# First weights in halves, squares shared with ScalarE, page numbers moved, and a new order at the end of the feed-forward: a one-core decoder layer

## What is computed

```python
xn = rms_norm(x, g)                       # x: 256 + 32 rows of 1024
z  = einsum('btd,de->bte', xn, w_in)      # the combined projection, then split into q, k, v, gates
...                                       # two attention branches over paged caches, found by page_table
h  = merge_branches(...)
hn = rms_norm(h, norm_ffn_g)
u, g = hn @ w_up, hn @ w_gate             # 3072 columns each
uc = conv_b + sum(conv_w[k] * ue[:, k:k + T] for k in range(3))
y  = h + (gelu(uc) * g) @ w_down          # out: y_prompt, y_sample
conv_rows = ue[:, -2:]                    # out: p_conv, s_conv, the last two rows of u
```

## Time and profile before

| | us |
|---|---|
| median of 3 runs (lowest, highest) | 930.73 (930.58, 931.37) |
| the profiled execution, its own time | 936.61 |
| its span, first to last instruction | 933.8 |
| PE busy in the span | 865.1 (93%) |
| DVE busy | 525.0 (56%) |
| ACT busy | 367.8 (39%) |
| GpSimd (POOL) busy | 160.9 (17%) |
| granted TensorE clock, mean over the span | 0.974 |

### The profile page before, as it was taken

How to read it: one execution, slowest core, us unless ns; L and a number is a source line. 1 busy time by engine, 2 the same in 40 slices (tenths; PEclk the granted TensorE clock), 3 DMA queues, 4 the chain that set the end, 5 groups by cost and what they waited for, 6 DMA issues and landing times. The chain is left out here.

```text
span 933.8 us, 18057 instructions
## 1 busy us (share of the span) xinstructions
PE 865.1 (93%) x7225; PEld 709.6 (76%) x7225; DVE 525.0 (56%) x981; ACT 367.8 (39%) x662; POOL 160.9 (17%) x262
## 2 busy tenths in 40 slices
PE   3999878799999999999999977999979999999996
PEld 2888667689989977655656455997678988989884
DVE  5466578633434566754467434656656655666554
ACT  3336565432434323453224422434144434444330
POOL 1200041311121022233434510000010110101000
PEclk9999989999999899999999999999979999999999
DMA  5543096165424269989999995974064444564412
GB/s 173 182 165 109 14 313 234 56 149 131 173 93 182 91 249 395 325 319 411 414 416 420 385 407 155 300 243 160 9 207 145 146 135 140 200 194 140 135 45 60
DMA packets 90608, 191.89 MB, mean 205 GB/s; under 512 B 7434, under 2 KB 68650, under 8 KB 78154
## 3 DMA queue, kind: packets, MB, share of 16 engines
q0 software_dynamic: 15408, 106.04, 29.3%
q1 hardware_dynamic: 73836, 84.43, 29.2%
q10 hardware_dynamic: 1296, 0.45, 0.2%
HBM read 187.44 MB, written 7.64 MB: 209 GB/s over the span
## 5 line engine op out<-in xcount | busy, mean ns | idle before, releaser
L1587 PEld LDWEIGHTS banks<-consts_base,stream_rows 128*128 128x128 f32 x672 | 73.2, 141 | 31.0 <-issue 27.3
L1834 ACT ACTIVATE keys_turned<-banks 128x512 f32<-128x512 f32 x94 | 54.9, 596 | 100.3 <-PE banks L1587 100.2
L258 PE MATMUL banks<-tokens_turned_high,w_gates_high 128*128 128x288 f32 x288 | 86.6, 301 | 3.5 <-PEq L191 2.3
L1587 PE MATMUL banks<-consts_base,stream_rows 128*128 128x128 f32 x672 | 82.5, 275 | 4.7 <-PEq L191 1.7
L259 PE MATMUL banks<-tokens_turned_low,w_gates_high 128*128 128x288 f32 x288 | 85.6, 297 | 0.0
L1126 PE MATMUL banks<-chunks_turned_high,cmp_w_high 64*128 64x256 f32 (+1 forms) x512 | 78.5, 300 | 5.3 <-DVE cmp_w_low L251 2.7
L260 PE MATMUL banks<-tokens_turned_high,w_gates_low 128*128 128x288 f32 x272 | 81.8, 301 | 0.0
L1126 PE MATMUL banks<-chunks_turned_low,cmp_w_high 64*128 64x256 f32 (+1 forms) x512 | 75.3, 288 | 0.0
L1126 PE MATMUL banks<-chunks_turned_high,cmp_w_low 64*128 64x256 f32 (+1 forms) x512 | 75.1, 287 | 0.0
L1815 DVE COPY keys_turned<-banks 128x512 f32<-128x512 f32 x74 | 50.4, 690 | 29.6 <-PE banks L1587 27.1
L251 DVE TENSOR_TENSOR chunks_turned_low<-banks,chunks_turned_high 128x512 fp32r<-128x512 f32 x64 | 41.1, 684 | 41.3 <-ACT chunks_turned_high L246 41.3
(11 more groups left out here) (446 smaller groups left out, 2110.1 us busy)
## 6 DMA issues: line engine op xcount, KB each, us to landing
w_up_gate<-in_w_up SPq DMA_DIRECT2D x12, 1024.0 KB, 7.4
w_up_gate<-in_w_gate SPq DMA_DIRECT2D x12, 1024.0 KB, 9.9
w_down<-in_w_down SPq DMA_DIRECT2D x12, 1024.0 KB, 5.0
w_in_slot<-in_w_in SPq DMA_DIRECT2D x8, 1424.0 KB, 6.3
w_gates<-in_w_in SPq DMA_DIRECT2D x10, 512.0 KB, 7.5
cmp_w<-in_cmp_w_k SPq DMA_DIRECT2D x4, 512.0 KB, 8.7
cmp_w<-in_cmp_w_v SPq DMA_DIRECT2D x4, 512.0 KB, 11.4
stream_rows<-in_state_win_k SPq DMA_DIRECT2D x8, 256.0 KB, 8.8
```

What stands on the lines that cost most here:

```text
L258: nc.tensor.matmul(out, lh, rh, start=start, stop=False, **kw)
L1587: ins = nc.tensor.transpose(bank(t)[:, q * P:(q + 1) * P], src, ident)
L1834: copy = lambda a, b: nc.scalar.activation(a, b, ACT.Copy)
```

## The change

1. Tokens: the squares of tiles 1 and 2 are made by ACT (Square with an accumulated sum) and those of tile 0 by DVE. ACT's order is squares 1, root 0, root 1, squares 2, root 2.
2. The first block of weights is loaded as two halves, and its high part is made at the start of the projection, by halves, each followed by DVE's low half.
3. The eight loads of page numbers go from ACT's list in the tokens stage to SP's in the projection, behind block 1.
4. End of the feed-forward: `down_sample` comes ahead of the last `down`; DVE adds each prompt tile as soon as its two banks are done, and SP stores it; the six groups of new rows go through six banks, and ACT copies four of them out.

```diff
@@ stage_tokens, sync
-            load_w_in(c, sp, w, w_loaded, 0, ORDER[0] * ZC)
+            for half in range(2):
+                src = c.d["w_in"].rearrange("l (k p) e -> p (l k) e", p=P)[:, half * KD // 2:(half + 1) * KD // 2, bass.ds(ORDER[0] * ZC, ZC)]
+                sp.dma_start(first_half(w[0], half), src).then_inc(w_first[half], 16)
@@ stage_tokens, scalar
-            with nc.allow_non_contiguous_dma(reason="1024 page numbers"):
-                for b in range(DB):
-                    src = bcast(d["page_table"][b, :], 1, 8)
-                    act.dma_start(c.pages[:, b:b + 1], src.unsqueeze(2)).then_inc(pages_in, 16)
-            for t in range(3):
-                act.wait_ge(squared, t + 1)
+            def squares(t):
+                act.wait_ge(tokens_in[t], 16)
+                nc.scalar.activation(xn[0:rows[t], t, :], x[0:rows[t], t, :], ACT.Square, scale=D ** -0.5,
+                                     accum_out=ss[0:rows[t], t:t + 1]).then_inc(squared[t], 1)
+            def root(t):
+                act.wait_ge(squared[t], 1)
                 nc.scalar.activation(ss[0:rows[t], t:t + 1], ss[0:rows[t], t:t + 1], ACT.Sqrt,
                                      bias=c.eps[0:rows[t], :]).then_inc(root_ready, 1)
+            act.wait_ge(eps_ready, 1)
+            squares(1)
+            root(0)
+            root(1)
+            squares(2)
+            root(2)
...
-            act.wait_ge(w_loaded[0], 16)
-            split_high(nc, wh[0][:, :, :], w[0][:, :, :]).then_inc(high, 1)
@@ stage_project, sync
             load_w_in(c, sp, w, w_loaded, 1, at(1))
+            with nc.allow_non_contiguous_dma(reason="1024 page numbers"):
+                for b in range(DB):
+                    src = bcast(d["page_table"][b, :], 1, 8)
+                    sp.dma_start(c.pages[:, b:b + 1], src.unsqueeze(2)).then_inc(c.pages_in, 16)
@@ stage_project, scalar
+            for half in range(2):
+                act.wait_ge(w_first[half], 16)
+                split_high(nc, first_half(wh[0], half), first_half(w[0], half)).then_inc((first_high, high)[half], 1)
@@ stage_project, vector
-            dve.wait_ge(high, 1)
             for half in range(2):
+                dve.wait_ge((first_high, high)[half], 1)
+                split_low(nc, first_half(wl[0], half), first_half(w[0], half), first_half(wh[0], half)).then_inc((first_low, low)[half], 1)
@@ stage_ffn, sync
+            for t in range(QT):
+                sp.wait_ge(y_ready, 2 * t + 2)
+                sp.dma_start(d["y_prompt"].rearrange("b (t p) d -> p (b t) d", p=P)[:, t, :], h[:, t, :]).then_inc(c.stored, 16)
             sp.wait_ge(y_ready, 6)
-            sp.dma_start(d["y_prompt"].rearrange("b (t p) d -> p (b t) d", p=P), h[:, 0:2, :]).then_inc(c.stored, 16)
@@ stage_ffn, tensor, after the loop
+            pe.wait_ge(dn_low, FT)
+            pe.wait_ge(hid_ready, FT)
+            down_sample(1, False)
             pe.wait_ge(hid_low, FT)
-            pe.wait_ge(dn_low, FT)
-            down(1, False)
-            down_sample(1, False)
+            down(1, False, rows_done)
...
             for g in range(FT // 4):
-                pe.wait_ge(kept, FT)
-                if g >= 2:
-                    pe.wait_ge(lcopy, g - 1)
+                if g in (2, 4):
+                    pe.wait_ge(y_ready, g)
                 for k in range(4):
-                    ins = nc.tensor.transpose(c.ps[g % 2][0:NL, k * P:(k + 1) * P], last[:, 4 * g + k, :], c.k("ident"))
+                    ins = nc.tensor.transpose(c.ps[g][0:NL, k * P:(k + 1) * P], last[:, 4 * g + k, :], c.k("ident"))
@@ stage_ffn, scalar, after the loop
+            for g in (0, 1, 2, 4):
+                act.wait_ge(lturn, g + 1)
+                nc.scalar.activation(last_rows[:, g * 512:(g + 1) * 512], c.ps[g][0:NL, :], ACT.Copy).then_inc(lcopy, 1)
@@ stage_ffn, vector
+                else:
+                    dve.wait_ge(rows_done, t + 1)
...
-            for g in range(FT // 4):
+            for g in (3, 5):
```

More of the change, by code:

```diff
@@ L273, in load_w_in, with first_half, stage_tokens @@
     sp.dma_start(w[u][:, :, :], c.d["w_in"].rearrange("l (k p) e -> p (l k) e", p=P)[:, :, bass.ds(start, ZC)]).then_inc(loaded[u], 16)
-def stage_tokens(c, z_at, w, w_loaded, wh, high):
+def first_half(x, half):
+    return x[:, half * KD // 2:(half + 1) * KD // 2, :]
+def stage_tokens(c, z_at, w, w_first):
     nc, d = c.nc, c.d
@@ L287, in stage_tokens @@
         high_ready = c.sem("xT_high_ready")
-        pages_in, squared, root_ready = c.pages_in, c.sem("x_squared"), c.sem("x_root_ready")
+        squared, root_ready, eps_ready = [c.sem(f"x_squared{t}") for t in range(3)], c.sem("x_root_ready"), c.sem("eps_ready")
         rows = [P, P, NS]
@@ L323, in _ @@
             link = c.chain(dve, "vector")
[L324 to L329, removed]
+            nc.vector.memset(c.eps[:, :], EPS).then_inc(eps_ready, 1)
+            dve.wait_ge(tokens_in[0], 16)
+            nc.vector.tensor_tensor_reduce(xn[:, 0, :], x[:, 0, :], x[:, 0, :], 1.0 / D, 0.0,
+                                           ALU.mult, ALU.add, ss[:, 0:1]).then_inc(squared[0], 1)
             dve.wait_ge(gain_in, 16)
@@ L356, with stage_project @@
 ORDER = (3, 4, 5, 6, 0, 1, 2, 7)
-def stage_project(c, z, w, w_loaded, wh, wl, high, chunks):
+def stage_project(c, z, w, w_first, w_loaded, wh, wl, chunks):
     nc, d = c.nc, c.d
@@ L377, in stage_project @@
         qgain = c.sb("q_gains_by_partition", [P, 2], ctx=ctx)
+        high, first_high = c.sem("w_in_high_ready"), c.sem("w_in_first_high_ready")
         low, first_low = c.sem("w_in_low_ready"), c.sem("w_in_first_low_ready")
+        loads = lambda n: 16 * (n // 2 + n % 2)
         z_out = [c.sem(f"z_copied_{e}") for e in "va"]
@@ L483, in _ @@
                     pe.wait_ge(fold_out, n - 1)
-                pe.wait_ge(w_loaded[u], n // 2 * 16 + 16)
+                if n:
+                    pe.wait_ge(w_loaded[u], loads(n))
                 for k in range(KD):
                     g = k % 4
+                    if n == 0 and k % 4 == 0:
+                        pe.wait_ge(w_first[k // 4], 16)
                     m = nc.tensor.matmul(U[3 * u + 2][32 * g:32 * g + 32, 0:ZC], c.xsT[:, k, :], w[u][:, k, :], start=(k < 4), stop=(k >= 4))
@@ L518, in split @@
                 u = n % 2
-                act.wait_ge(w_loaded[u], n // 2 * 16 + 16)
+                act.wait_ge(w_loaded[u], loads(n))
                 if n >= 2:
@@ L2529, in _, with down @@
             loop(sp, FT // 4, body)
+            for t in range(QT):
+                sp.wait_ge(y_ready, 2 * t + 2)
+                sp.dma_start(d["y_prompt"].rearrange("b (t p) d -> p (b t) d", p=P)[:, t, :], h[:, t, :]).then_inc(c.stored, 16)
             sp.wait_ge(y_ready, 6)
-            sp.dma_start(d["y_prompt"].rearrange("b (t p) d -> p (b t) d", p=P), h[:, 0:2, :]).then_inc(c.stored, 16)
             sp.dma_start(d["y_sample"].rearrange("b s d -> (b s) d"), h[0:NS, 2, :]).then_inc(c.stored, 16)
-            sp.wait_ge(lcopy, FT // 4)
+            sp.wait_ge(lcopy, 4)
+            sp.wait_ge(lcopy_late, 2)
             sp.dma_start(d["p_conv"].rearrange("l b w f -> (l b w) f"), last_rows[0:2, :]).then_inc(c.stored, 16)
             sp.dma_start(d["s_conv"].rearrange("l b w f -> (l b w) f"), last_rows[2:NL, :]).then_inc(c.stored, 16)
-            sp.wait_ge(c.stored, 16 * (c.n_stored + 4))
+            sp.wait_ge(c.stored, 16 * (c.n_stored + 5))
         @block.tensor
         def _(pe):
-            def down(f, start):
+            def down(f, start, rows_done=None):
                 for t in range(QT):
@@ L2546, in down @@
                                       start=start, stop=True, skip_group_check=True)
-                ins.then_inc(down_done, 1)
+                    if rows_done:
+                        ins.then_inc(rows_done, 1)
+                if not rows_done:
+                    ins.then_inc(down_done, 1)
             def down_sample(u, start):
@@ L2772, in build @@
                     wl = [c.at("w_in_low0", [P, KD, ZC], F32R, 8 * NH * SEQ), c.in_big("w_in_low1", [P, KD, ZC], F32R, 0)]
-                    w_loaded, high = [c.sem(f"w_in_loaded{u}") for u in range(2)], c.sem("w_in_high_ready")
-                    stage_tokens(c, z_at, w, w_loaded, wh, high)
-                    stage_project(c, z, w, w_loaded, wh, wl, high, chunks)
+                    w_loaded, w_first = [c.sem(f"w_in_loaded{u}") for u in range(2)], [c.sem(f"w_in_first_loaded{u}") for u in range(2)]
+                    stage_tokens(c, z_at, w, w_first)
+                    stage_project(c, z, w, w_first, w_loaded, wh, wl, chunks)
                 stage_prompt(c, z, chunks)
```

6 lines of the change are left out of this document (3 added, 3 removed).

## The result

| | before | changed |
|---|---|---|
| median of 20 runs, taken together (lowest, highest) | 931.66 (930.58, 936.35) | 937.20 (931.67, 939.51) |
| ratio of the times, 95% interval | | 1.0031 (1.0018 to 1.0043) |
| the profiled execution, own time | 936.61 | 937.52 |
| its span | 933.8 | 935.8 |
| PE busy | 865.1 | 866.6 |

The changed kernel is slower by 0.31%, 2.9 us of 932, where 929.6 was forecast. Its median is outside the range, and the sign is the other one. The sign is sure and the size less so: over these 20 runs of each the means differ by 3.7 and the medians by 5.5, because the times of the kernel before fall in two groups (of 35 runs taken together, 13 took 930.16 to 932.54 and 22 took 934.42 to 937.17, with none between), and a median depends on how many runs fell in which. The three runs shown ahead of the prediction are all in the range of the lower group.

A forecast was written before the change was run, and what follows sets the result against it. PE's path, block 2's chain to the row numbers close behind it, and DVE's path to the last store bound the kernel. Front +1.5 and end -2.6 made -1.1, from 930.73 to 929.6; range 927.2 to 932.4.

The forecast's parts named there:

- What bounds the kernel: Whole program: PE, busy 93% of the span, bounds it; only its path or the path to the last store counts.
- the front: Program start through PE's wait for block 2's row numbers: forecast to lose 1.5, numbers at 44.9 instead of 43.38.
- Part 1, the squares: Tokens stage: two table loads behind tile 1's landing (7.3), first root about 11.4; DVE ends 1.8 later, at 18.86.
- The rival of an emptied ACT: Tokens stage: draining ACT before each table load takes some 1.4 twice, block 2's chain 2.8 later, 932.4; chance 0.02.
- Part 2, the weights: Projection start: stage ends at 19.6, 0.9 earlier; PE's products start at 22.6 against 23.07, gaining 0.45.
- Part 3, the page numbers: SP's queue in the projection: small transfers hold 0.44 each; block 2 lands at 38.8, 2.6 later; PE loses 1.5.
- The clock: Behind PE's new stop of about 2.0: a low stretch costs 0 to 2.5, taken as 1.7, giving 931.3; chance 0.25.
- the bare forecast: Whole program: 929.6, from +1.5 and -2.6, without any rival's term; chance 0.45.
- The drained queue: SP's queue: small transfers served while it is filled, block 2 before 37.3, PE never stops, 927.2; chance 0.22.
- The held queue at 1.0 each: SP's queue: page numbers hold it 1.0 each, block 2 lands at 43.4, PE 6.1 late, 934.2; chance 0.06.
- Part 4, the end: End of the feed-forward: last copy ends at 926.8 instead of 929.44, gaining 2.6 (2.2 to 2.8).
- The base: Whole program: median 930.73 of the runs before, to which the -1.1 was carried over from the profiled execution.

The follow-up runs named there:

- experiment 2: Kernel before with only the changed end of the feed-forward stage; ratio to before 0.9973 (0.9953 to 0.9993).
- Experiment 5: Changed kernel with page numbers back on ACT's queue and all squares back on DVE; ratio to before 0.9929 (0.9907 to 0.9951).
- Experiment 9: Changed kernel with PE's stop ahead of the row numbers filled by 17 unused products; ratio to before 0.9986 (0.9967 to 1.0005).
- Experiments 7 and 8: 7: changed kernel, page-number loads issued twice, second eight into a spare buffer; 1.0081 to before. 8: changed kernel, page-number loads behind block 2 on SP's queue; 0.9972.
- experiment 3: Changed kernel with the eight page-number loads back on ACT's queue ahead of the squares; ratio to before 0.9975 (0.9956 to 0.9994).
- experiment 6: Changed kernel plus an early root of eps ahead of ACT's squares, removing the extra table load; ratio to before 1.0002 (0.9986 to 1.0018).
- the front alone: Changed kernel with the feed-forward stage of before; ratio to before 1.0058 (1.0037 to 1.0078).

## Why the prediction was wrong

In the traces -1.1 was forecast and +2.0 came. Of the 3.1 between, 1.8 is block 2's landing, which the sum of part 3 put too early, and 1.6 is the low clock, which the sum had at nothing; the end gave back 0.4, and 0.1 is what lies between.

- **What bounds the kernel: right.** PE's path, the chain from block 2's landing to the row numbers, and the path to the last store explain what the traces show. The row that the prediction began with says little of the front, though: the chain of the profile's page covers 26% of the span, and it was the timelines that showed the front.
- **Part 1, the squares: the mechanism right, a landing mis-sized.** Two table loads behind tile 1 and 4.1 to the root came as worked out. But the landing was read from one execution (7.3) and was 8.23 in this one. Such small landings differ from run to run: the first reciprocal is at 9.64 in before and at 10.24 in the kernel of experiment 2, with the same front. So the start was 0.95 late: 20.57 for 19.6. The rival of an emptied ACT is excluded: the second load starts 0.02 behind the read of the sum.
- **Part 2, the weights: right from the start on.** Full products came 3.1 behind the start of the projection, for 3.0, so at 23.69 and not 22.6 because of the late start alone. Experiment 5 shows 1.3 of gain there once the squares are back on DVE.
- **Part 3, the page numbers: the step that failed.** Its sum put block 2's landing at 38.8; it was 40.50. Block 1's data ended at about 26.2 and not 25.4 (0.8, the late start again), and the sixteen small transfers took 8.5 from there and not 7.0 (0.53 each for 0.44); the data then took 0.6 less to land. The landing-to-numbers chain was 6.1, as taken. That makes PE 3.3 late at the row numbers instead of 1.5. The term was counted from the wrong event: the prediction had the issue of block 2 nearly right (30.5; it was 31.13), but let the data follow it by 1.9, where its own rows had 3.9 and the changed kernel has 3.5. Its issue at 30.5 and the 10.3 from issue to landing of the kernel before give 40.8, within 0.3 of what was measured.
- **The clock: a term that the sum had at nothing, and a rival with 0.25 that came true.** A stop of 2.21 lowered it, as the one of 2.92 had, and the clock was low for 3.4, which cost 1.6. The rival's term was 1.7, picked inside 0 to 2.5 with no row for it, so that it is so near is luck. Experiment 9 shows the price with a stop that is filled. The front's 4.9 is the 1.5 that was forecast, 1.8 of the later landing and 1.6 of the clock. Each rival stood against the bare forecast, and no case had a later landing and the low clock together, though the one makes the other likelier.
- **The drained queue: excluded, and the rule beside it misread.** Block 2 landed at 40.50 and not before 37.3. Experiments 7 and 8 show small transfers that delay what stands behind them and do nothing to what stands ahead, and by experiment 3 the same loads on ACT's queue are free, because ACT would only wait for tile 1 in that time (8.23 in the changed kernel). The Trainium skill's page "DMA: Bandwidth & Descriptors", section "Issuing engines are not separate DMA queues", says that starting transfers on another engine only saves the sequencer's time to start them. The prediction took that for this rival; but SP's time to issue, 5.35 for the eight, is what moved block 2's issue by 5.2, and the landing by 4.3. These traces agree with the rule, and what it leaves out is that the sequencer's time can be on the critical path. The held queue at 1.0 each is excluded by 0.53 and 0.69, though the landing did pass the 39.9 from which that rival was said to decide.
- **Part 4, the end: right**, 3.0 in the trace and 2.5 (0.7 to 4.4) timed, for 2.6.
- **The base.** The forecast hung on three runs with times of the lower group. In a ratio it would have said 0.999 for 1.0031.

## What to carry to other kernels

Before moving small loads to an engine that looks idle, list what it has to issue behind them: each of these made the next large load land some 0.5 to 0.7 us later, about its own time to issue, and the same loads behind the large one, or on a queue with nothing urgent after them, cost nothing. A new wait of PE costs its own length and can cost the low clock behind it (not behind 1.37 here, but behind 2.12 and more); price both from the start, and fill the stop or move another piece of work ahead of it. When an engine takes over an activation ahead of one that needs another table, start once, early, with the one whose table serves both (here Sqrt), and first look whether some other landing (here the gain's) sets the stage anyway.

## What was not expected of the hardware

- **Stops.** A stop of 2.21, 2.12 (experiment 6) or 2.42 (the front alone) between work at the full clock is followed by 3.4 at half the clock, with PE busy. Behind 0.45, 0.86 and 1.37 the clock stayed at 1.00. One trace of each is all there is.
- **The clock recorded at the start is not to be relied on.** In experiment 3 a window reads 1.00 while full products stand 0.50 long until 28.44, as at the low clock, and 0.32 from 28.71 on:

```profile
24.00:28.00 4.00, 4.00 (x15) 4.00 (x15) 1.17 (x2) 1.56 (x1) 3.82 (x7) 1.00 0.54 178
```

```profile
27.25 0.50 PE L259 MATMUL banks<-w_in_low,tokens_turned_high 128*128 128x356 f32 x1
...
28.71 0.32 PE L258 MATMUL banks<-w_in_high,tokens_turned_high 128*128 128x356 f32 x1
```

  When the products became short varied from 24.8 to 28.7 over the traced executions. At half the clock that is up to some 1.9 of time (an estimate from these two places).
- **The two groups of times.** They are groups of the clock too: of the 35 runs of the kernel before, the 13 below 933 have a mean granted clock of 0.980 to 0.987 and the 22 above 934 one of 0.972 to 0.980. The traces show one place for it. Before and the change each have, near 300 us, a low stretch with PE busy throughout; the executions of experiments 3 and 7 do not have it, and those two (929.19 and 938.78) are among the shortest of their kernels. It is low for 6.8 in before, which takes 3.4, near the distance of the groups. Windows of the changed kernel, of before and of experiment 3:

```profile
308.00:313.00 5.00, 5.00 (x44) 4.96 (x45) 0.00 (x0) 0.00 (x0) 0.00 (x0) 0.50 0.00 0
```

```profile
302.50:308.50 6.00, 6.00 (x50) 5.96 (x52) 0.00 (x0) 0.00 (x0) 0.00 (x0) 0.50 0.00 0
```

```profile
304.00:308.00 4.00, 4.00 (x60) 3.86 (x57) 0.00 (x0) 0.15 (x1) 0.00 (x0) 1.00 0.00 0
```

  Two traced executions without the stretch are no proof that it makes the groups, and what calls it forth, with PE busy ahead of it, stays open.
